# Two transformer blocks on one core: longer runs of dense products, head pairs dealt 3 + 1, and 64-row products in pairs

## The reference, cut to what matters

```python
h = rmsnorm(x, g); u = h @ w_in                    # RWKV, attention and gate columns
o_a = rwkv7_time_mix(u_rwkv)                       # 8 heads of 64, a recurrence over tokens
o_b = diff_attention(u_attn)                       # 4 heads, two score maps each, 64 deep
merged = g_a * (o_a @ w_proj_a) + g_b * (o_b @ w_proj_b)
x = x + merged @ w_out
x = x + relu(rmsnorm(x) @ w_ff1)**2 @ w_ff2
x = x + (p @ w_ple) * sigmoid(rmsnorm(x) @ w_ple_gate)
```

## Time and profile before

| | us |
|---|---|
| median of 3 runs | 1956.66 (1953.95 to 1958.48) |
| the profiled execution | 1953.57 |
| its span, first to last instruction | 1951.8 |
| PE busy | 1928.2 (99%) |
| DVE busy | 1017.2 (52%) |
| ACT busy | 738.6 (38%) |
| mean granted TensorE clock | 0.997 |

### The profile page before, as it was taken

One profiled execution on the slowest core, in us unless ns is written; L12 is line 12 of the kernel. 1 busy time (PEld: TensorE's weight loads), 2 busy tenths in 40 slices (PEclk: granted clock), 3 DMA queues, 4 the chain that ended last, 5 costly groups with the idle time before them and its releaser, 6 DMA issues.

```text
span 1951.8 us, 23333 instructions
## 1 busy us (share of the span) xinstructions
PE 1928.2 (99%) x9550; PEld 1580.0 (81%) x9550; DVE 1017.2 (52%) x1717; ACT 738.6 (38%) x1184; POOL 99.9 (5%) x155
## 2 busy tenths in 40 slices
PE   7999999999999999999999999999999999999997
PEld 6787778778888888888788888898888888888886
DVE  5768574446754444466834435424345644444544
ACT  6434454333433223234734233333233432313233
POOL 2000111102000000000101000000000000000000
PEclk9999999999999999999999999999999999999999
DMA  6232310226343233232432222231354332322321
GB/s 223 65 103 95 82 46 29 65 76 234 102 149 99 96 97 98 96 99 76 142 98 64 74 80 84 91 107 64 110 194 141 97 108 87 108 86 87 108 87 43
DMA packets 174557, 194.65 MB, mean 100 GB/s; under 512 B 14825, under 2 KB 151699, under 8 KB 174450
## 3 DMA queue, kind: packets, MB, share of 16 engines
q1 hardware_dynamic: 167794, 179.82, 28.8%
q0 software_dynamic: 5072, 11.03, 1.7%
q10 hardware_dynamic: 1584, 2.30, 0.3%
HBM read 179.41 MB, written 15.54 MB: 100 GB/s over the span
## 4 chain that ended last, share of the span: by engine, by line
PE 95%; DVE 2%; ACT 2%; DMA 1%; issue 0%; POOL 0%; ACTq 0%; POOLq 0%; DVEq 0%
PE bank L130 93%; PE bank L133 2%; ACT L140 0%; DMA scr_x<-XT 0%; DVE XL L162 0%; DVE XT L162 0%; ACT GP L140 0%; DVE wl L154 0%; DMA g_rows<-in_norm_mix_g_dram 0%; ACT xt L140 0%; DVE KI L154 0%; DVE GP L162 0%; ACT LD L140 0%; DVE GP L177 0%; POOL scr_x L118 0%
## 5 line engine op out<-in xcount | busy, mean ns | idle before, releaser
L140 ACT ACTIVATE wh<-raw 128x1024 fp32r<-128x1024 f32 (+1 forms) x299 | 316.0, 1057 | 709.7 <-PE bank L130 706.0
L130 PE MATMUL bank<-XH,wh 128*128 128x512 f32 (+1 forms) x1272 | 507.7, 399 | 3.0 <-DVE XL L162 2.2
L130 PE MATMUL bank<-XL,wh 128*128 128x512 f32 (+1 forms) x1272 | 497.0, 391 | 0.0
L154 DVE TENSOR_TENSOR wl<-raw,wh 128x1024 fp32r<-128x1024 f32 x298 | 365.2, 1226 | 228.6 <-ACT wh L140 227.9
L130 PE MATMUL bank<-XH,wl 128*128 128x512 f32 x1264 | 324.3, 394 | 0.0
L130 PEld LDWEIGHTS bank<-XH,wh 128*128 128x128 f32 (+1 forms) x1272 | 239.1, 188 | 60.4 <-issue 5.2
L130 PEld LDWEIGHTS bank<-XL,wh 128*128 128x128 f32 (+1 forms) x1272 | 239.2, 188 | 47.9
L130 PEld LDWEIGHTS bank<-XH,wl 128*128 128x128 f32 x1264 | 233.5, 188 | 51.9 <-issue 4.1
L130 PE MATMUL bank<-mid,wh 128*128 128x512 f32 x1024 | 243.8, 389 | 0.0
L130 PEld LDWEIGHTS bank<-mid,wh 128*128 128x128 f32 x1024 | 192.2, 188 | 39.9
L154 DVE TENSOR_TENSOR T<-bank,RST 128x512 f32<-128x512 f32 x122 | 84.1, 689 | 234.2 <-PE bank L130 234.0
(11 more groups left out here) (426 smaller groups left out, 2319.3 us busy)
## 6 DMA issues: line engine op xcount, KB each, us to landing
raw<-in_w_in_dram SPq DMA_DIRECT2D x58, 1024.0 KB, 5.3
raw<-in_w_ff_dram SPq DMA_DIRECT2D x32, 1024.0 KB, 5.3
raw<-in_w_mlp_dram SPq DMA_DIRECT2D x32, 1024.0 KB, 5.3
raw<-in_w_out_dram SPq DMA_DIRECT2D x8, 1024.0 KB, 5.6
scr_x<-XT POOLq DMA_DIRECT2D x16, 256.0 KB, 4.9
XT<-scr_x SPq DMA_DIRECT2D x8, 512.0 KB, 8.0
raw<-in_w_ple_gate_dram SPq DMA_DIRECT2D x4, 1024.0 KB, 5.3
raw<-in_w_o_gla_dram SPq DMA_DIRECT2D x4, 1024.0 KB, 5.3
```

What stands on the lines that cost most here:

```text
L130: return self.put(ns, lambda e: e.matmul(out, lhsT, rhs, start=start, stop=stop, skip_group_check=True))
L140: return self.put(ns, lambda e: e.activation(out, in_, func, bias=bias, scale=scale), func)
L154: return self.put(self.ns(out), lambda e: e.tensor_tensor(out, a, b, op))
```

## The change

Six edits, the first three in what the planner may do:

- Dense steps are twice as long: `upper` yields every fourth k, `under` every eighth, so a run of dense products can be left after 8 of them.
- `PATIENCE`: where the last TensorE step was dense and dense can go on, it goes on as long as no helper step has been ready for its lane's patience: 2000 ns for scores and sums, 4000 ns for the second block's helpers, 0 for RWKV. The planner also adds 90 ns to its clock when it goes from dense to helpers or back.
- `WORK` deals three head pairs (0, 1, 3) to worker 0 and one (2) to worker 1.
- `pe_scores` takes both maps in one step: c = 0 into bank 6 and c = 1 into bank 2, after both `mx` of the step before. `dv_scores` reads the two banks.
- Bank 2 is therefore taken out of the dense ring (two banks, 0 and 1) from the end of `av` to the first `OB` tile: 20 output tiles.
- c2 of a worker's half is one step: it waits for `akr` of both heads, and issues p = 0 of both heads, then p = 1 of both.

In the whole order there are then 120 excursions instead of 174, and 243 changes of tile size instead of 288; the instructions are the same, 7264 dense and 1332 others.

```diff
-WORK = ((0, 1), (2, 3))
+PATIENCE = (2000, 4000, 0)
+WORK = ((0, 1, 3), (2,))
...
-        b = self.dense_i % 3
+        b = self.ring[self.dense_i % len(self.ring)]
...
-            if k % 2 == 0 and k > k0:
+            if k % 4 == 0 and k > k0:
                 yield
...
-            if k % 4 == 0:
+            if k % 8 == 0:
                 yield
...
         yield from self.tm(s, "X0", ("av",), [("begin", 3)])
+
+        assert self.last_use[2] == [self.SCORES_FROM]
+        self.ring, self.last_use[2] = (0, 1), [("mx", 3, 3, 1)]
...
             if pr >= 0:
+                self.ring = (0, 1, 2)
                 yield from self.fm(s, "OB", ("pb", 2 * pr), ("pb", 2 * pr + 1))
...
-            for h, bank in enumerate((B0, B1)):
-                yield
-                rows = slice(64 * h, 64 * h + 64)
-                pe.wait_ge(at("akr", *me, h))
-                for p in range(2):
+            yield
+
+            pe.wait_ge(at("akr", *me, 0), at("akr", *me, 1))
+            for p in range(2):
+                for h, bank in enumerate((B0, B1)):
+                    rows = slice(64 * h, 64 * h + 64)
                     t = pe.matmul(bank[:, 128 * p:128 * p + 128], BT[rows, col(p)], AR[rows, 1, col(p)], p == 0, True)
-                t.then_inc(*s.up(("c2", *me, h)))
+                    if p:
+                        t.then_inc(*s.up(("c2", *me, h)))
...
-        last = [("begin", 6)]
+        last = [("begin", 6), self.SCORES_FROM]
         for h, b in self.items:
             n = 128 * (b + 1)
+            yield
+            qk = self.AQ[h % 2]
+            pe.wait_ge(self.at("free", "aqk", 1, h), self.at("free", "aqk", 0, h), *[self.at(*e) for e in last])
             for c in range(2):
-                yield
-                rows, qk = slice(64 * c, 64 * c + 64), self.AQ[h % 2]
-                pe.wait_ge(self.at("free", "aqk", 1, h), self.at("free", "aqk", 0, h), *[self.at(*e) for e in last])
+                rows, bank = slice(64 * c, 64 * c + 64), self.ps[(6, 2)[c]]
                 pe.matmul(bank[:, 0:n], qk[rows, 0, 128 * b:128 * b + 128], qk[rows, 1, 0:n], True, True).then_inc(*s.up(("sc", h, b, c)))
-                last = [("mx", h, b, c)]
+            last = [("mx", h, b, 0), ("mx", h, b, 1)]
...
+            if eng == "pe":
+
+                was = self.order[eng][-1] if self.order[eng] else lane
+                dense_lane = [l for _, l in go if l.name == "dense"]
+                if was.name == "dense" and dense_lane and all(start - t < l.patience[l.i] for t, l in go if l.name != "dense"):
+                    lane = dense_lane[0]
             now, stream = start, streams[eng]
+            if eng == "pe" and (lane.name == "dense") != (was.name == "dense"):
+                now += 90
```

More of the change, by code:

```diff
@@ L223, in __init__ @@
         self.stream, self.name, self.write, self.slack = stream, name, write, slack
-        self.steps, self.unit_of, self.i, self.gen = [], [], 0, None
+        self.steps, self.unit_of, self.patience, self.i, self.gen = [], [], [], 0, None
 class Kernel:
@@ L1041, in pe_prep @@
     def pe_prep(self, s, i):
+        self.patient = PATIENCE[2]
         pe, bank = self.pe, self.ps[4 + i % 2]
@@ L1204, in pe_worker @@
     def pe_worker(self, s, w):
+        self.patient = 0
         pe, b, at = self.pe, self.W[w], self.at
@@ L1507, in pl_group_norm @@
             pl.power(st[2][:, :], st[1][:, :], self.mhalf[:, 0:4]).then_inc(*pl.mark(s, ("gr", i, hf)))
+    SCORES_FROM = ("free", "av", 0)
     def attn_pages(self, h, b):
@@ L1531, in pe_scores @@
     def pe_scores(self, s):
-        pe, bank = self.pe, self.ps[6]
-        last = [("begin", 6)]
+        pe = self.pe
+        self.patient = PATIENCE[0]
+        last = [("begin", 6), self.SCORES_FROM]
         for h, b in self.items:
             n = 128 * (b + 1)
+            yield
+            qk = self.AQ[h % 2]
+            pe.wait_ge(self.at("free", "aqk", 1, h), self.at("free", "aqk", 0, h), *[self.at(*e) for e in last])
             for c in range(2):
-                yield
-                rows, qk = slice(64 * c, 64 * c + 64), self.AQ[h % 2]
-                pe.wait_ge(self.at("free", "aqk", 1, h), self.at("free", "aqk", 0, h), *[self.at(*e) for e in last])
+                rows, bank = slice(64 * c, 64 * c + 64), self.ps[(6, 2)[c]]
                 pe.matmul(bank[:, 0:n], qk[rows, 0, 128 * b:128 * b + 128], qk[rows, 1, 0:n], True, True).then_inc(*s.up(("sc", h, b, c)))
-                last = [("mx", h, b, c)]
+            last = [("mx", h, b, 0), ("mx", h, b, 1)]
     def dv_scores(self, s):
-        dv, bank = self.dv, self.ps[6]
+        dv = self.dv
         for x, (h, b) in enumerate(self.items):
@@ L1547, in dv_scores @@
             for c in range(2):
+                bank = self.ps[(6, 2)[c]]
                 yield
@@ L2357, in pe_gla_prep @@
         pe = self.pe
+        self.patient = PATIENCE[1]
         yield
@@ L2867, in rehearse @@
             for name, slack, write in lanes():
-                self.splitting = 0
+                self.splitting = self.patient = 0
                 lane = Lane(eng, name, write, slack)
@@ L2879, in rehearse @@
                     lane.unit_of.append(self.splitting)
+                    lane.patience.append(self.patient)
                 self.lanes.append(lane)
```

## The result

The changed kernel took **1931.43 us** (median of 4 runs, 1930.35 to 1932.75), the kernel before 1957.13 (4 runs, 1953.95 to 1958.48): a ratio of 0.9874, 95% interval 0.9858 to 0.9889. Forecast were 1937.0 us and a range of 1931 to 1945.5: the measured time lies 0.4 us above its lower end, and outside the 1933 to 1940 that had most of the chance. The profiled executions took 1930.49 and 1953.57 us, 23.1 apart, where the sum of the steps was 19.7.

A forecast was written before the change was run, and what follows sets the result against it. PE's own instruction stream was taken to set the end. Savings of 8.6 + 0.3 + 8.4 + 2.4 = 19.7 us off the 1956.66 us median gave 1937.0 us, range 1931 to 1945.5.

The forecast's parts named there:

- an outcome of 2 to 5 more: Whole launch: gain exceeds the sum by 2 to 5 us if unseen small stalls go; chance 0.03.
- Tile-size changes: PE's order: 45 fewer changes of tile size at 0.19 us each save 8.6 us, bounds 6.3 to 9.0.
- Scores in pairs: Score products on PE: the second map runs beside the first in other rows, saving 8.4 us, bounds 0 to 8.5.
- c2: RWKV c2 products: both heads in one step run side by side, saving 2.4 us, bounds 0 to 2.6.
- Fewer excursions beyond: PE leaving dense work: 54 fewer excursions, full-size ones worth 0.01 us each way, save 0.3 us, bounds 0 to 0.5.
- Ring: Two dense banks: each is read within the next tile's 5.5 us, so PE waits 0 us.
- End of the chain: From `GD,G2` to the last `OAL`, 1.9 us: 10 dense products, 2.3 us, still cover it, so 0.
- Links: RWKV chain links on PE: uncovered ones cost 0.5 us; 5 if a quarter of some 50 fell short.
- the scores don't overlap: Rival, score pairs: no overlap gives 1945.4 us, half of it 1941; chance of no or half an overlap 0.12.
- covers too thin: Rival: chain links fall short or DVE makes banks wait, price 5 to 6 us, 1942.5 us; chance 0.11.
- Worker 0 can't finish: Rival: worker 0's six halves exceed 36.3 us each, PE idles, slower than before beyond 40.3; chance 0.02.
- a clock below full in a slice: Profile after: a granted clock below full in any slice would show the prediction wrong; no size given.

The follow-up runs named there:

- e5: The changed kernel with no patience for the second block's helpers; median 1932.51 us.
- e7: The kernel before with nothing but the ring of two dense banks; median 1956.97 us, ratio 1.0005.
- e9: The changed kernel with both maps' score products reading the same rows 0 to 63, still in two banks; median 1939.78 us.
- e2: The kernel before with the planner's part alone (longer dense steps, patience, 90 ns), deal 2 + 2; median 1960.42 us, ratio 1.0027.
- e10: The kernel before with the planner's part and the 3 + 1 deal of head pairs, scores and c2 as before; median 1948.19 us.
- e1: The kernel before with both score maps in one step and the ring of two banks, nothing else; median 1943.15 us, ratio 0.9935.
- e3: The changed kernel with the head pairs dealt 2 + 2 as before; median 1937.54 us.
- e11: The changed kernel with y-step products grouped by size and both heads' c1 products in one step, rows alternating; median 1923.25 us, ratio 0.984.

## Why the prediction was right

The forecast held since each step was read from distances between ends on PE's timeline, and the stretch gave what the sum said: 19.9 us for 19.7. That the two agree to 0.2 is luck in part: the single terms differ by up to 1.5 us and offset each other. And the launch became 25.7 us shorter by the medians, 6 more than the sum, where an outcome of 2 to 5 more had a chance of 0.03 from me; the paragraph on profile and median below says where that comes from.

- **Tile-size changes, 8.6.** Returns to dense products gave 7.7 - 1.8 = 5.9 us for 28, 0.21 each, and the score entries 2.7 for 16, 0.17 each; together 8.6. With the c2 entries it is about 1.1 more, 9.7. Against it stand entries that are new: in the trace `G,NB` and `ident,AP` each follow a record of another size three times more often, `ident,SQ` twice. So 28, 16 and 6 fewer, and 4 fewer ahead of `AR,KT`, come to 45 with some 9 new ones, and at 0.19 these are 1.7 of the 2.5 us by which all others rose. Right in price, and in the balance.
- **Scores in pairs, 8.4.** Measured by its removal: 8.5 in the score products, 7.6 in the whole stretch. The doubt was whether two halves wider than 256 columns run side by side. They do, up to 512. My estimate from the Trainium skill, "TensorE: Matmul & The Clock Gate", Part 3 (measured speedup), was 5.9 us and 1939.5: the trace disagrees with the estimate. A 512-wide product adds 0.01 us beside another in the other rows and 0.85 in the same rows, so the streaming of two takes as long as that of one, and nothing of the share 0.77 is seen. That page's figure is of four row tiles, though, and no run here has four, so the figure itself is not contradicted.
- **c2, 2.4.** `AR,BT` fell by 3.7: that is the 2.6 of six halves side by side, and 1.1 for six entries at 0.19, which the prediction had among its changes. Taking the edit back cost 4.8, with returns and 0.4 of idle time.
- **Fewer excursions beyond, 0.3.** Within the stretch this can't be told apart. Behind it the step failed: "nothing should move by more than a microsecond" held by a hair (1.0), but with 0.01 us for an excursion of full size 14 fewer would have given 0.1 (measured on average 0.11 in e5, 1.0 / 14 = 0.07 here). The earlier trace rows show one excursion; what the others lose is open.
- **Ring, 0.** Right (e7). **End of the chain, 0.** Right in the result: no wait there. But only with the deal; with 2 + 2 it is 4.8 us of waiting.
- **Links, 0.5 uncovered.** The changed kernel's new waits are 0.5 us. The others in the table rose by 2.5 (`G,NB` 0.65, `ident,AP` 0.56, `SB,MP` 0.5 the most): these waits, and the new entries above.
- **Not in the sum: c1, 1.5.** The two heads' c1 steps stand together more often and run side by side; 4 fewer entries, some 0.8, are in it too. The prediction saw this for `AR,BT` in the earlier trace rows and did not look at `AR,KT`, which has the same form.

The rivals: "the scores don't overlap" is refuted by the pair e9 and after; "covers too thin" describes e2, the planner without the deal, though its cause there was not DVE's reading of banks but the last half without company. So the Trainium skill's PSUM Bottleneck ("TensorEngine Tiling (Array Packing)") didn't act here: no wait of PE of over 0.15 us in the changed kernel is for a score bank, and e7 shows none on the ring. "Worker 0 can't finish" stayed away with 35.8 us a half, 0.5 below its threshold. That makes the 0.02 I gave it look too sure.

Do the parts add up? Planner and deal 3.7 (e10), pairs and c2 on top of them 312.2 - 296.0 = 16.2. For the latter the prices say 8.5 for the pairs, 2.6 for c2 and 28 changes x 0.19 = 5.3: 16.4. For e1 they say 39 x 0.19 + 8.5 = 15.9 less 0.9 of new idle time, 15.0; measured 14.1, and there c2's two heads stand together in one half instead of two and `AR,BT` takes 1.7 us more (10.3 against 8.7). For e2, 14 x 0.19 = 2.7 gained against 9.2 lost in waits would be +6.5; measured +5.5. The 1 us left may be c1 steps that came together: `AR,KT` has 7.0 us there against 8.75.

**Profile against median.** The medians differ by 25.7 us, the profiled executions by 23.1. I had taken the median of the kernel before as reference, 3.1 above its profiled execution, without knowing what the 3.1 were. The runs tell it in part: see the last section. With 19.7 off the profiled time, 1933.9, the forecast for an execution like the one read was nearer to what came (1930.49); of the 3.4 that are left, 2.1 are PE's idle time at the start, which follows no edit, and 1.0 the time behind the stretch.

**The clock.** "The granted clock is full in all 40 slices, so 2.4 GHz throughout" read too much into the digits, where a 9 is 90% or more of a slice of 49 us. The profiled execution of the kernel before has a window at 1.2 GHz near its start:

```profile
13.10:16.50 3.40, 3.22 (x8) 2.57 (x9) 3.40 (x6) 3.40 (x7) 0.00 (x0) 0.50 1.10 324
```

So has that of the changed kernel, at 14.6. Both lie outside the stretch, and nothing of the sum hangs on them. But the sign "a clock below full in a slice" could not have shown a window as short as that.

## What to carry to other kernels

Where PE is busy 99% of the time and nothing waits, price a change by ends on PE's timeline: here a change of tile size cost 0.14 to 0.21 us wherever it stood, and a product in the other 64 rows, writing another bank, was free next to its twin. Then look for every such pair, not only those that the change speaks of: the y step and c1 gave 12.5 us in the kernel before by reordering the products of two steps, about half of what the whole change gave. And longer runs of dense work are only a gain if something is left beside the last link of the longest chain; look at the end of that chain first.

## What the runs showed of the hardware

**The granted clock falls for some microseconds in some executions.** In the kernel with the ring of two banks PE was never idle, and still (stretch: length, busy us and records of PE, PEld, DVE, ACT, POOL, granted clock, DMA):

```profile
262.00:268.00 6.00, 6.00 (x74) 4.68 (x72) 3.92 (x15) 2.28 (x8) 0.00 (x0) 1.00 0.16 46
268.00:276.40 8.40, 8.40 (x58) 5.72 (x57) 5.75 (x23) 5.66 (x11) 1.01 (x1) 1.00 0.00 0
276.40:286.60 10.20, 10.20 (x40) 6.86 (x40) 3.62 (x9) 2.81 (x5) 2.69 (x6) 0.50 0.40 130
```

The last window is at 0.50, 1.2 GHz; the stretch as it ran is 4.6 us longer than that of the kernel before. Ahead of it PE had worked mostly on short helper products, 10.3 of the 14.4 us by ends. The kernel before has nearly the same order, 10.2 us of helpers in the same 14.4, and its clock stayed at full there in its profiled execution. The same happened in e1 at 289.4, behind another row of helpers:

```profile
282.00:289.40 7.40, 7.33 (x106) 5.83 (x106) 4.77 (x11) 2.49 (x5) 0.00 (x0) 1.00 0.33 109
289.40:296.20 6.80, 6.80 (x38) 5.27 (x38) 1.73 (x6) 1.04 (x3) 1.73 (x6) 0.50 0.00 0
```

In e2 it fell at 452.8, behind 6.8 us without a dense product and with idle links; in e3 at 437.2, within the wait of 4.8 us.

That fits the medians. Of the 47 executions of the kernel before that ran beside the experiments, the 25 at a mean granted clock of 0.997 or more took 1951.88 to 1956.66 us (median 1953.2), the 22 at 0.996 or less 1955.20 to 1962.38 (median 1957.1). The four of the changed kernel are all at 0.997 or 0.998 (1930.35 to 1932.75), those of the planner alone all at 0.993 to 0.995. Like against like, 1953.2 against 1931.4, the change is worth some 22 us; of the 25.7 between the medians some 2.5 are that the changed kernel, in the executions seen, kept its clock and the kernel before in about half of them didn't, and 1.5 that the four of the kernel before beside it stand above the median of all 51, 1955.7. What decides about the clock in an execution no run here shows.

**Row halves and column halves.** Products with 64 rows each that write different banks overlapped in full at 128 columns (c1, c2) and up to 512 (scores). Score products of 64 rows by 128 columns that lie in the same rows didn't overlap at all, in one bank or in two (e9). With tiles of 64 by 64 the columns count too: the c1 products of one head lie in the same 64 rows and the same bank, and only the halves of the columns differ. Their records start in pairs 0.007 us apart (238.779 and 238.786), and eight of them take 0.65 us, less than four records of c2, which are as wide (0.71). With both heads, in e11, four start within 0.02 us of each other (241.732 to 241.752), and 16 take 0.67 us: four tiles at once. No run here has two score products in different rows that write one bank, so whether they need two is open.
